# Two weighing and copying steps of an attention moved between VectorE, ScalarE and GpSimd

## What is computed

```python
s = jnp.einsum('bqkgd,bskd->bkgqs', q, k, preferred_element_type=jnp.float32) * (q.shape[-1] ** -0.5)
p = jax.nn.softmax(s, axis=-1).astype(v.dtype)
return jnp.einsum('bkgqs,bskd->bqkgd', p, v)
# neighbourhood heads of the latents: a bias and a mask on 256 of the 512 scores
s_lat = jnp.where(valid[:, :, None, :], s_lat + bias.astype(jnp.float32), NEG_INF)
```

## Time and profile before

| | us |
|---|---|
| median of 3 runs | 2115.83 (2115.69 to 2124.15) |
| the profiled execution, its own time | 2117.01 |
| its span in the profile | 2115.70 |
| PE busy | 2074.0 (98%) |
| DVE busy | 1216.8 (58%) |
| ACT busy | 808.9 (38%) |
| POOL busy | 57.1 (3%), 58 instructions |

### The profile page before, as it was taken

The page is one execution under the profiler, slowest core; times in us unless marked ns, Lnnn a source line. Parts: engine busy times, 40 slices in busy tenths (PEclk is TensorE's granted clock), DMA queues, the critical chain, the costliest instruction groups (busy, mean ns, idle before and its releaser), DMA issues.

```text
span 2115.7 us, 35529 instructions
## 1 busy us (share of the span) xinstructions
PE 2074.0 (98%) x15250; PEld 1772.6 (84%) x15250; DVE 1216.8 (58%) x1842; ACT 808.9 (38%) x1183; POOL 57.1 (3%) x58
## 2 busy tenths in 40 slices
PE   8999999999999999999999999999999999989998
PEld 8886899998888888866888888888888888769998
DVE  6756765766565546775654333465453346867665
ACT  6433544553222234256432222343222234465444
POOL 0000300000000000400000000000000000200000
PEclk9999999999999999999999999999999999999999
DMA  8627755453354325244233332233353225315553
GB/s 335 229 83 247 252 186 194 162 183 131 125 184 149 117 83 130 89 140 160 100 125 129 99 112 84 77 136 137 125 184 100 87 83 142 138 59 174 179 172 114
DMA packets 86269, 303.38 MB, mean 143 GB/s; under 512 B 14192, under 2 KB 41200, under 8 KB 65392
## 3 DMA queue, kind: packets, MB, share of 16 engines
q1 hardware_dynamic: 86128, 301.34, 42.2%
HBM read 300.26 MB, written 1.05 MB: 142 GB/s over the span
## 4 chain that ended last, share of the span: by engine, by line
PE 87%; DVE 8%; ACT 3%; issue 1%; DMA 1%; SPq 0%; ACTq 0%; DVEq 0%
PE ps L544 25%; PE ps L546 25%; PE ps L545 25%; DVE w_lo L531 2%; PE ps L2360 1%; PE ps L576 1%; DVE a_lo L1656 1%; PE ps L2649 1%; PE ps L2609 1%; PE ps L2637 1%; DVE mx L2742 1%; ACT a_hi L1505 1%; ACT ee L2690 1%; ACT pt L2703 1%; DMA raw<-in_w_ada 1%
## 5 line engine op out<-in xcount | busy, mean ns | idle before, releaser
L544 PE MATMUL ps<-a_hi,w_hi 128*128 128x512 f32 (+2 forms) x2136 | 729.5, 342 | 2.8 <-DVE w_lo L531 1.4
L545 PE MATMUL ps<-a_lo,w_hi 128*128 128x512 f32 (+2 forms) x2136 | 725.2, 339 | 0.0
L546 PE MATMUL ps<-a_hi,w_lo 128*128 128x512 f32 (+2 forms) x2136 | 725.1, 339 | 0.0
L531 DVE TENSOR_TENSOR w_lo<-raw,w_hi 128x2048 fp32r<-128x2048 f32 (+1 forms) x227 | 467.8, 2063 | 121.4 <-ACT w_hi L525 120.9
L525 ACT ACTIVATE w_hi<-raw 128x2048 fp32r<-128x2048 f32 (+1 forms) x227 | 387.5, 1712 | 182.9 <-PE ps L546 170.2
L544 PEld LDWEIGHTS ps<-a_hi,w_hi 128*128 128x128 f32 x2136 | 404.5, 189 | 52.1 <-issue 6.1
L546 PEld LDWEIGHTS ps<-a_hi,w_lo 128*128 128x128 f32 x2136 | 404.5, 189 | 44.5
L545 PEld LDWEIGHTS ps<-a_lo,w_hi 128*128 128x128 f32 x2136 | 404.6, 189 | 44.0
L544 PE MATMUL ps<-ff_hi,w_hi 128*128 128x512 f32 (+1 forms) x880 | 306.4, 348 | 0.6 <-DVE ff_lo L1153 0.3
L545 PE MATMUL ps<-ff_lo,w_hi 128*128 128x512 f32 (+1 forms) x880 | 305.1, 347 | 0.0
L546 PE MATMUL ps<-ff_hi,w_lo 128*128 128x512 f32 (+1 forms) x880 | 305.0, 347 | 0.0
(11 more groups left out here) (444 smaller groups left out, 1977.3 us busy)
## 6 DMA issues: line engine op xcount, KB each, us to landing
raw<-in_w_gu SPq DMA_DIRECT2D x110, 1024.0 KB, 4.9
raw<-in_w_dn SPq DMA_DIRECT2D x80, 704.0 KB, 4.1
raw<-in_w_ada SPq DMA_DIRECT2D x48, 1024.0 KB, 5.5
raw<-in_w_in SPq DMA_DIRECT2D x24, 1024.0 KB, 6.4
row_w<-in_w_ada SPq DMA_DIRECT2D x48, 512.0 KB, 5.9
raw<-in_w_out SPq DMA_DIRECT2D x12, 1024.0 KB, 5.0
direct<-in_w_cmp SPq DMA_DIRECT2D x4, 1024.0 KB, 8.9
raw<-in_w_in SPq DMA_DIRECT2D x4, 512.0 KB, 7.7
```

The source lines that it names most:

```text
L531: nc.vector.tensor_tensor(w_lo[slot][:, cols], raw[b][:, cols], w_hi[slot][:, cols].bitcast(F32), ALU.subtract).then_inc(lo_ready if done ...
L544: nc.tensor.matmul(banks[m], w1, a1, start=start and k == 0, stop=False)
L545: nc.tensor.matmul(banks[m], w1, a2, start=False, stop=False)
L546: last = nc.tensor.matmul(banks[m], w2, a1, start=False, stop=stop and k == pr.kt - 1)
```

## The change

In the stages of layers 0 and 1:

- the weighing of jobs 2 and on goes from DVE to POOL: DVE keeps the reciprocal and raises the new semaphore `at_fac`; POOL (`pool_weigh`) multiplies both heads' exponentials in place and raises `at_norm` after each;
- the copy of the second head's transposed probabilities (`par == 1`) goes from ACT to DVE (`dve_turned`), except in bias jobs; in DVE's list it stands behind the maximum of job t and ahead of the reciprocal of job t-1;
- `at_pt` becomes one semaphore for each head.

The first attention (`key == "first"`) keeps its work where it was.

```diff
+    at_pt = [sem(f"at_pt{par}") for par in range(2)]
+    at_fac = sem("at_fac")
...
+    def copied_by_dve(key, x, par):
+        return key != "first" and par == 1 and not x.scaled
...
                 pe.wait_ge(at_norm, 2 * j + par + 1)
-                wait(pe, at_pt, 2 * (j - 1) + par + 1)
+                wait(pe, at_pt[par], j)
...
-            pe.wait_ge(at_pt, 2 * j + 2)
+            for par in range(2):
+                pe.wait_ge(at_pt[par], j + 1)
...
         def turned(t, par):
             j, x = j0 + t, jobs[t]
+            if copied_by_dve(key, x, par):
+                return
...
+    def dve_turned(dve, key, t):
+        _, jobs, j0 = stage_of[key]
+        j, x = j0 + t, jobs[t]
+        if copied_by_dve(key, x, 1):
+            dve.wait_ge(at_trans, 2 * j + 2)
+            wait(dve, at_pv, j - 1)
+            nc.vector.tensor_copy(pt[j % 2][:, 1, 0:x.width], turn_bank(key, 1)[:, 0:x.width]).then_inc(at_pt[1], 1)
+
+    def weighed_by_pool(key, t):
+        return key != "first" and t >= EARLY_JOBS
+
+    def pool_weigh(pool, key, before):
+        _, jobs, j0 = stage_of[key]
+        for t in range(EARLY_JOBS, len(jobs)):
+            j, x = j0 + t, jobs[t]
+            pool.wait_ge(at_fac, before + t - EARLY_JOBS + 1)
+            for par in range(2):
+                e = probs(key, t, j)[:, par, 0:x.width]
+                nc.gpsimd.tensor_scalar(e, e, fac[:, 2 * t + par, 0:1], None, ALU.mult).then_inc(at_norm, 1)
...
     def dve_weigh(dve, key, u, step):
...
         dve.wait_ge(at_exp, j + 1)
+        if weighed_by_pool(key, u):
+            V.reciprocal(per_seg(fac, u, x), per_seg(sm, u, x)).then_inc(at_fac, 1)
+            return
...
             else:
+                if t < n + 2:
+                    dve_turned(dve, key, t - 2)
                 if first < t < n + 1:
                     dve_weigh(dve, key, t - 1, step)
                 lower(t)
...
             pool_mix(pool, l)
+            pool_weigh(pool, l, l * (len(stage_of[0][1]) - EARLY_JOBS))
```

More of the change, by code:

```diff
@@ L2509, in program @@
     at_trans = sem("at_trans")
-    at_pt = sem("at_pt")
+    at_pt = [sem(f"at_pt{par}") for par in range(2)]
+    at_fac = sem("at_fac")
     at_pv = sem("at_pv")
@@ L2702, in turned @@
             w = 512 if x.segs == 2 else x.width
-            nc.scalar.activation(view(pt[j % 2][:, par, 0:w]), view(turn_bank(key, par)[:, 0:w]), ACT.Copy).then_inc(at_pt, 1)
+            nc.scalar.activation(view(pt[j % 2][:, par, 0:w]), view(turn_bank(key, par)[:, 0:w]), ACT.Copy).then_inc(at_pt[par], 1)
         for t in range(n + 5):
```

## The result

| | before | after |
|---|---|---|
| median of 4 runs, us | 2116.06 (2115.69 to 2124.15) | **2145.86** (2139.56 to 2147.34) |
| the profiled execution, us | 2117.01 | 2145.16 |
| its span, us | 2115.70 | 2143.9 |

The ratio is 1.0129, 95% interval 1.011 to 1.0149: the changed kernel is 1.3% slower. The forecast was 2119 and the range ended at 2130; the result lies outside it, on the side to which I had given a chance of 0.21.

A forecast was written before the change was run, and what follows sets the result against it. PE was taken to bound the kernel, busy for 98% of the span. Layer 1 +2.2, layer 0 -0.3 and the lock +1.0 gave +2.9 us on 2117.01; the median lies 1.2 lower: 2119, range 2112 to 2130.

The forecast's parts named there:

- the side to which I had given a chance of 0.21: Whole kernel slower by over 0.5%, that is above 2126.4 us; chance 0.21.
- the price of POOL's half: One head's multiplication by its factors on POOL in the attention stages: 0.80 us at 512 columns, 0.45 at 256.
- The bracket: Bounds for one POOL multiplication of 512 columns: 0.61 us from its one-input copy, 1.1 from its two-input sum.
- The chain: Per job: transposes, DVE's copy, reciprocal, two POOL multiplications, next transposes; 3.3 us at 512 keys, 2.1 at 256.
- The opening: Start of both stages: copies ahead of the reciprocal delay job 2's transposes, +1.7 us in layer 1, 2.1 in layer 0.
- Part of the slow stretch then falls into that wait: Layer 0's start: low-clock time overlaps PE's longer wait, so only +0.3 us is charged, 2.1 as upper end.
- Middle and end: Layer 1: bias jobs -0.2, jobs 6 to 9 -0.6, end +1.3 us; layer 0: jobs 6 to 11 -0.3.
- ACT's loop of 7.66: Mid-stage two-job turn between ACT and DVE, 7.66 us before; forecast to fall to 6.7, with POOL's two jobs at 6.6.
- The clock falls in layer 1 too: Rival: longer waits at layer 1's start bring a slow stretch costing 2.9 to 5 us, 2122 to 2124; chance 0.13.
- POOL becomes the bound: Rival: at 1.1 us a multiplication, 3.9 us a job in both stages; +10, 2126, then 2 us per 0.1; chance 0.22.
- DVE's order: DVE's list in the stages puts a PE wait ahead of each reciprocal; named against a gain, no separate size.
- The lock: Both stages: DVE's tiny `nm` late by up to 0.8 us behind POOL in a third of jobs; +1.0 us, 0 to 3.

The follow-up runs named there:

- the first and the third experiment: First: the change with all copies back on ACT, 2128.96 us (1.0059). Third: the change with the reciprocal ahead of the copy in DVE's list, 2126.53 (1.0033).

## Why the prediction was wrong

**The step that failed** is the price of POOL's half: "I take 0.80, just under the middle, since it is nearer to the copy in what it reads". It measured 1.56. The bracket itself was false: its upper end of 1.1 came from a two-input sum, on the idea that an operation that reads less cannot take longer. The run with two inputs shows that this idea is wrong here, 1.04 with a second input and 1.49 with a constant and none. The Trainium skill (GPSIMD Engine Reference, "Performance versus the Vector engine") gives 769 ns for 512 elements, as its best case; the trace does not agree for this operation, which took 1562 ns. I had let rows of other operations, both cheap, stand as a bound on one that the trace did not hold. That this step made the miss is shown by the runs that moved the price alone: with a half at 0.61 the same kernel is at 2113.6, at 1.04 at 2123.4, and between them, by interpolation at my 0.80, at 2118, near the forecast of 2119.

**The chain** was right in its members, and mis-sized by that one term: 3.3 us a job forecast, 4.71 measured; 2 x (1.56 - 0.80) = 1.5 makes up the difference, with 0.1 less for the rest.

**The opening.** For layer 1 I had +1.7 and for layer 0 2.1 until job 2's transposes. Measured from the stage's first scores: layer 1 from 7.68 to 10.09 (+2.4), layer 0 from 9.32 to 11.76 (+2.4). With 0.76 more for the first half, layer 1's 1.7 would have been 2.5. "Part of the slow stretch then falls into that wait", by which I took only +0.3 in layer 0, came out about so. The clock was low there again, at 0.60 between 924 and 930, but the value product and the scores alone ran into it, at 1.98 and 2.08, where before a job's transposes, values and scores had. Job 3's transposes, which follow job 2's, started 16.31 us behind the stage's first scores before

```profile
932.29 1.09 PE L2637 MATMUL ps<-consts_sb,ee 128*128 128x128 f32 x8
```

and 16.98 with the change:

```profile
933.01 0.66 PE L2641 MATMUL ps<-consts_sb,ee 128*128 128x128 f32 x4
```

So layer 0 was only 0.7 behind by then. Layer 1 was 5.5 behind at the same job (17.63 for 12.16): there the clock had been at 1.00 before and fell with the change.

**Middle and end.** I gave back 0.2, 0.6 and 0.3 where two turns of the chain fitted under ACT's loop of 7.66. Two turns of 4.71 do not. The transposes of jobs 9 and 10 stand 4.7 apart at the end of layer 1 in place of 2.9.

**The clock.** "The clock falls in layer 1 too" had 0.13 and came true: 0.84 over the stage in place of 1.00. On PE's path I count 1.8 us behind the first wait (1.98 and 2.08 for 1.09 and 1.13), 1.6 in the stretch at 1894 to 1899, and 2.2 at the end (1.11 for 0.66, 3.68 for 1.97), 5.6 us, just above the 2.9 to 5 of that rival. In the one kept trace of each version it went with the longer waits: with halves of 1.04 the clock of layer 1 stayed at 1.00, with halves of 1.49 it fell to 0.91, and with those of 1.56 but without the chain, in the first and the third experiment, to 0.93 and 0.97. So I take it as a consequence of the price and not as a cause of its own; no run holds the clock fixed.

**The bound.** The rival "POOL becomes the bound" had the right mechanism, and its 2126 at 1.1 us fits the 2123.4 measured at 1.04. Its slope beyond was too flat: "beyond it 2 us for each 0.1" gives 2126 + 4.6 x 2 = 2135, and 2140 with the clock; measured 2145.9. The runs show about 4. The jobs were counted rightly: jobs 2 to 5 stay near PE's own 4.1 us, and only the later 512-wide ones, about ten in both layers, run at the chain's pace, as here in layer 0 (1.60 idle and 3.10 busy make 4.70):

```profile
957.97 3.10 POOL L2775 TENSOR_SCALAR ee<-ee,fac 128x512 f32<-128x512 f32 x2 [1.60 <-DVE fac L2783]
```

Between halves of 1.04 and of 1.56 the two stages grew by 20.2 us in the kept traces. Ten jobs with two halves of 0.52 more are 10.4 of these. The 256-wide jobs, which the slope had left out, add about 3 by the starts of their transposes, and the low clock of layer 1 the 5.6 counted above. That split is a count on two traces, not a measurement: of the 20.2 us PE is idle for 7.6 and busy for 12.6, and no run tells how much of either the clock makes.

**Whether DVE's order matters.** The forecast named it as what stands against any gain, "which puts a PE wait ahead of each reciprocal", and costed it only inside the chain. It is the larger part: 19 of the 30 us.

**The lock** was put at 1.0 us for both layers: the tiny `nm`, which reads `mx` and `rn`, was to stand behind a POOL half, by up to 0.8 us. That did not happen. All 24 of them in the changed kernel (count, ns min/median/max):

```profile
L2751 DVE SCALAR_TENSOR_TENSOR nm<-mx,rn x24: 160/161/210, 909.5 to 1902.5; 128x2 f32<-128x2 f32 x24
```

The median is 161 ns as before, and the longest is late by 0.05 us. Eleven of the 24 lay wholly inside a half on POOL, ten of these at 160 to 163 ns and one at 210. One of the ten on DVE's timeline

```profile
1902.49 0.16 DVE L2751 SCALAR_TENSOR_TENSOR nm<-mx,rn 128x2 f32<-128x2 f32 x1
```

lies wholly inside a pair of halves on POOL's, with no delay:

```profile
1900.11 3.10 POOL L2775 TENSOR_SCALAR ee<-ee,fac 128x512 f32<-128x512 f32 x2 [1.72 <-DVE fac L2783]
```

So this term is 0, and `nm` is not an instruction that POOL locks out, though it has two SBUF inputs. The Trainium skill (SBUF — State Buffer, "Who interferes with whom") has a DVE instruction with two SBUF inputs contend with a POOL instruction that reads SBUF, and the engine that issues first keep the shared port for its whole instruction. The trace does not agree for `nm`, 128x2. For DVE's multiplication of 512 columns, which reads one SBUF tensor and the column of factors, the runs show the waiting: 1.36 in place of 0.49, or 1.86 on POOL in place of 1.56. There the trace agrees that one engine waits for the other; but DVE had to wait even where its recorded start was 0.04 us earlier.

## What to carry to other kernels

Before work moves to an engine, find a row of that very form of operation on that engine, or take its price as unknown upwards; a row with more inputs is no upper bound. Then write down the turn of the loop that the move creates, in the order of each engine's list, and ask whether anything in it waits for a later stage's result: here a copy ahead of a reciprocal joined a harmless move and one that cost 12 us into one chain of 4.7 us a job, and exchanging them gave back two thirds of the loss. Where a time is a sum of maxima, a price error costs little while there is cover and the whole of it in every job once the cover is gone, so give the far side of the range the steeper slope.

## What the runs showed of the hardware

- On POOL, in place on 128 partitions of float32: copy 0.61 us at 512 columns (0.40 at 256), product of two inputs 1.04 (0.61), product with a constant 1.49 (0.85), with a factor for each partition 1.56 (0.92). On DVE the last takes 0.49.
- DVE's multiplication and POOL's, both with SBUF operands and started within 0.06 us of each other, ran nearly one behind the other: 0.49 and 1.86, or 1.36 and 1.04, where alone they take 0.49 and 1.56 or 1.04. The 128x2 instruction `nm` inside a POOL half was not delayed, but for one of eleven by 0.05 us. DVE's copies from PSUM were not either: with half the weighing on POOL, 23 of 28 lay wholly inside a POOL half and took at most 0.69 us. A wait that puts POOL behind made the kernel faster.
- The 95% intervals were 0.1 to 0.2% to either side; the 0.5% that the prediction took as the least to be told apart was cautious.
